# Layer 0 of a hybrid decoder step as one stream of weight products, with the delta-rule heads in between and no products inside a pair of heads

## The reference, cut to what matters

```
qkv, z, b_raw, a_raw, lx, ly = jnp.split(hn @ w_in, cuts, axis=-1)
qkv, qkv_buf_new = _causal_conv(qkv, qkv_buf, conv_qkv_w)
qkv = jax.nn.silu(qkv)
q = _l2norm(qkv[..., :GDN_QK]...) * (GDN_DK ** -0.5)
k = _l2norm(qkv[..., GDN_QK:2 * GDN_QK]...)
beta = jax.nn.sigmoid(b_raw);  g = -jnp.exp(a_log) * jax.nn.softplus(a_raw + dt_bias)
o, s_new = _gated_delta(q, k, v, beta, g, s0)
o = _rmsnorm(o, gdn_norm_g) * jax.nn.silu(z)
xb, lru_buf_new = _causal_conv(lx, lru_buf, conv_lru_w)
r = sigmoid(einsum(xblk, lru_wa) + lru_ba);  ig = sigmoid(einsum(xblk, lru_wi) + lru_bi)
log_a = -LRU_C * r * jax.nn.softplus(-lru_lambda);  a = jnp.exp(log_a)
bt = jnp.sqrt(-jnp.expm1(2.0 * log_a)) * (ig * xb)
hs = scan of h = a * h + bt;   ob = hs * jax.nn.gelu(ly)
mix = jnp.concatenate([o, ob], axis=-1) @ w_out
```

## Time and profile before

| what | value |
|---|---|
| median of 3 runs (lowest to highest) | 3324.95 us (3315.17 to 3325.36) |
| the profiled execution's own time | 3318.15 us |
| its span | 3316.3 us |
| PE busy / PEld busy | 3094.3 us (93%) / 2930.9 us (88%) |
| DVE busy / ACT busy | 1615.5 us (49%) / 1108.6 us (33%) |
| bytes moved | 456.37 MB, mean 138 GB/s |
| layer 0's mixer on PE, first product to last | 30.9 to about 866 us |

### The profile page before, as it was taken

One profiled execution on the slowest core, in us unless ns is written; L12 is line 12 of the kernel. 1 busy time (PEld: TensorE's weight loads), 2 busy tenths in 40 slices (PEclk: granted clock), 3 DMA queues, 4 the chain that ended last, 5 costly groups with the idle time before them and its releaser, 6 DMA issues.

```text
span 3316.3 us, 53710 instructions
## 1 busy us (share of the span) xinstructions
PE 3094.3 (93%) x22096; PEld 2930.9 (88%) x22096; DVE 1615.5 (49%) x1733; ACT 1108.6 (33%) x1064; POOL 110.5 (3%) x130
## 2 busy tenths in 40 slices
PE   8998649988999999999999789989999999999997
PEld 7998527768999999999999788659999999999997
DVE  5655345555644444444456543445644444444454
ACT  4323420113343333333344222333333333333343
POOL 0000000001100000000002000001100000000012
PEclk9999856779999999999999888999999999999998
DMA  6444300114555555555554242435555555555552
GB/s 189 152 141 147 95 13 27 28 40 144 151 165 165 165 165 164 164 164 165 165 163 154 84 147 61 133 104 175 149 165 165 165 165 165 164 165 164 165 165 78
DMA packets 455650, 456.37 MB, mean 138 GB/s; under 512 B 22313, under 2 KB 440170, under 8 KB 455229
## 3 DMA queue, kind: packets, MB, share of 16 engines
q1 hardware_dynamic: 455118, 455.07, 45.6%
q10 hardware_dynamic: 450, 0.16, 0.0%
HBM read 446.97 MB, written 8.22 MB: 137 GB/s over the span
## 4 chain that ended last, share of the span: by engine, by line
PE 84%; DVE 8%; ACT 4%; issue 2%; DMA 1%; SPq 1%; DVEq 0%; ACTq 0%; POOL 0%; POOLq 0%
PE ps L1238 82%; PE ps L1245 2%; ACT Wh L1268 2%; DVE Wl L1643 1%; DVE acc L1745 1%; DVE TT L1924 0%; SPq L450 0%; SPq L468 0%; DMA hrow<-in_state_lru_conv 0%; DMA gw<-in_lru_wi 0%; DMA W<-in_w_o_c 0%; DVE S L1947 0%; DVE hT L1672 0%; DVE rB L1679 0%; DVE ple L1994 0%
## 5 line engine op out<-in xcount | busy, mean ns | idle before, releaser
L1643 DVE TENSOR_TENSOR Wl<-W,Wh 128x2048 fp32r<-128x2048 f32 (+2 forms) x408 | 910.4, 2233 | 1101.5 <-ACT Wh L1268 1101.5
L1268 ACT ACTIVATE Wh<-W 128x2048 fp32r<-128x2048 f32 (+2 forms) x408 | 757.7, 1860 | 1170.8 <-PE ps L1238 1164.3
L1238 PE MATMUL ps<-Ah,Wh 128*128 128x288 f32 x3344 | 990.7, 296 | 25.2 <-DVE Wl L1643 20.2
L1238 PE MATMUL ps<-Al,Wh 128*128 128x288 f32 x3344 | 989.5, 296 | 0.0
L1238 PE MATMUL ps<-Ah,Wl 128*128 128x288 f32 x3344 | 989.5, 296 | 0.0
L1238 PE MATMUL ps<-Bh,Wh 128*128 128x288 f32 x2704 | 798.7, 295 | 10.8 <-DVE Bl L1965 10.3
L1238 PE MATMUL ps<-Bl,Wh 128*128 128x288 f32 x2704 | 799.9, 296 | 0.0
L1238 PE MATMUL ps<-Bh,Wl 128*128 128x288 f32 x2704 | 799.9, 296 | 0.0
L1238 PEld LDWEIGHTS ps<-Ah,Wh 128*128 128x128 f32 x3344 | 629.1, 188 | 30.6 <-DVE Wl L1643 30.1
L1238 PEld LDWEIGHTS ps<-Al,Wh 128*128 128x128 f32 x3344 | 630.0, 188 | 0.3
L1238 PEld LDWEIGHTS ps<-Ah,Wl 128*128 128x128 f32 x3344 | 629.4, 188 | 0.3
(11 more groups left out here) (395 smaller groups left out, 2432.6 us busy)
## 6 DMA issues: line engine op xcount, KB each, us to landing
W<-in_w_up SPq DMA_DIRECT2D x128, 1024.0 KB, 5.9
W<-in_w_down SPq DMA_DIRECT2D x128, 1024.0 KB, 5.4
W<-in_w_in_a SPq DMA_DIRECT2D x48, 1024.0 KB, 5.4
W<-in_w_ple_gate SPq DMA_DIRECT2D x32, 1024.0 KB, 5.4
W<-in_w_out_a SPq DMA_DIRECT2D x16, 1024.0 KB, 5.4
CK<-in_cache_ckv SPq DMA_DIRECT2D x64, 256.0 KB, 2.5
W<-in_w_o_c SPq DMA_DIRECT2D x16, 1024.0 KB, 5.5
W<-in_w_ukv SPq DMA_DIRECT2D x12, 1024.0 KB, 5.5
```

Source lines behind the costliest of these rows:

```text
L1238: return m.nc.tensor.matmul(out, w, x, start=start, stop=stop)
L1268: last = A(x, w, ACT.Copy)
L1643: last = TT(low, w, f(high), SUB)
```

## The change

Layer 0 becomes one list of units, `UNITS`: LX, LY, BA, then Q, K, V, Z of each pair of heads, CS (transposes of the convolution states, without a weight slot), OL (the recurrent half of `w_out`, k tiles 8 to 15) and OG (the delta-rule half, k tiles 0 to 7). On PE, ACT and DVE a generator `stream()` runs through it; one tick is six products with what belongs to them on the other engines, and `fill(n)` issues the next n ticks. All else of layer 0 stands between calls of `fill`. `TICKS` says how many ticks stand behind each step of a pair: none but at its end, `ds=57`. The whole is 532 ticks.

What comes with it: every unit of the stream uses banks 6 and 7, and PE waits for the evacuation of the unit before (`evacuated(i - 1)`); OG alternates as before. The gate matrices and `cst0` are loaded at the start, all at once. `hT` is written to DRAM (2.36 MB) at the start and read back behind slot 52, because other tiles take its place. The l2 norm is made per pair (4 rows). The staging copy of q, k, v of a pair falls away, and so does one matmul with its copy (`BB`). The scaling of `S8` and of `vb` moves from DVE to ACT, 16 small `ACTIVATE` for `S8` in each pair. DVE's split is cut in two halves of 1024. `w_out` is done in two halves, each added to `hT`. Loops over heads are written out.

```diff
+def layer0_units():
+    units, slot = [], 0
+    order = [("LX", n, 2) for n in range(4)] + [("LY", n, 2) for n in range(4)] + [("BA", 0, 2)]
+    order += [(kind, t, 2) for t in range(4) for kind in "QKVZ"]
+    order += [("CS", n, 0) for n in range(4)] + [("OL", n, 1) for n in range(8)] + [("OG", n, 1) for n in range(8)]
+    ...
+TICKS = dict(tr=0, gram=0, t1=0, q=0, tb=0, v0=0, s1=0, x1=0, v1=0, s2=0, ds=57)
...
 # PE
-    k16(S_QKV, 0, *A, m.fl_done, 0, norm=0)
-    with pe.Fori(1, 6) as t:
-        k16(S_QKV, t, *A, None, 0)
-    with pe.Fori(0, 2) as t:
-        k16(S_Z, t, *A, None, 0)
-    one_tile(S_BA, *A, None, 0, 64, 40)
-    for S in (S_LX, S_LY):
-        with pe.Fori(0, 2) as t:
-            k16(S, t, *A, None, 0)
+    def stream():
+        for i, (kind, n, s, slots) in enumerate(UNITS):
+            b, (Xh, Xl), k0, kn = 6, A, 0, 16
+            ...
+            if kind == "OG":
+                b = 2 * ((n + 1) % 2)
+                ...
+            elif i:
+                evacuated(i - 1)
+            ...
+            for half in range(slots):
+                pe.wait_ge(m.split_done, s + half + 1)
+                ...
+                for k in range(8):
+                    ...
+                    for o in range(tiles):
+                        last = products(...)
+                    if k == 7:
+                        last.then_inc(m.slot_used, 1)
+                    yield
+    fill = filler(stream())
+    fill(64)
+    fill(8)
+    pe.wait_ge(m.gw_full, 32)
+    for k in range(8):
+        ...
+        if k >= 2:
+            pe.wait_ge(m.gate_act, k - 1)
+        for g in range(2):
+            last = mm(ps[:, 2 * (k % 2) + g, 0:NT], m.gw[:, k, g, :], m.xb[:, k, :], True, True)
+        last.then_inc(m.gate_mm, 1)
+        if k % 2:
+            fill(4)
+    fill(40 + 16)
+    ...                       # lo transposed, fill(12), gate scalars transposed
+    fill(4 + 16 + 16 + 9)
...
+    def l2_norm(t):
+        pe.wait_ge(m.l2_sq, t + 1)
+        head_sums(m.sqg, (0, 1, 8, 9)).then_inc(m.l2_sum, 1)
+        fill(2)
+        fill(3)
+        pe.wait_ge(m.l2_ref, t + 1)
+        ...                   # four rows to all partitions
+        fill(2)
...
-    with pe.Fori(0, HG // 2) as t:
-        heads(t)
+    l2_norm(0)
+    for t in range(4):
+        heads(t)              # fill(TICKS[...]) behind each step, fill(57) behind the last
+        if t < 3:
+            l2_norm(t + 1)
...
+    head_sums(m.sqo, range(HG)).then_inc(m.on_sum, 1)
+    fill(11)
+    pe.wait_ge(m.on_ref, BASE["on_ref"] + 1)
...
-    k16(S_OUT, ...)           # four turns over all 16 tiles of k
+    fill(48)
+    ple_turn(0)
+    fill(16)
 # ACT, heads(t)
+        for x, P, R, Q, g, sc in both:
+            for b in range(BS):
+                at = SEQ + TS * b + TS - 1
+                last = A(g.S8[:, b, :], g.S8[:, b, :], ACT.Copy, scale=g.Eb[:, at:at + 1])
+            last.then_inc(m.g_s8, 1)
 # ACT, gates and RG-LRU
+        if k % 2:
+            fill(4)
     act.wait_ge(m.lm_done, BASE["lm_done"] + 1)
     A(m.la[:], m.lm[:, 0], ACT.Exp, scale=-1.0)
     A(m.lt[:], m.lm[:, 0], ACT.Tanh).then_inc(m.lat_done, 1)
+    fill(8)
     act.wait_ge(m.lt_done, BASE["lt_done"] + 1)
     A(m.lt[:], m.lt[:], ACT.Sqrt).then_inc(m.lroot_done, 1)
 # SP, in states()
+        small(m.gw[:, :, 0, :], a["lru_wa"][0].rearrange("k p n -> p k n"), m.gw_full)
+        small(m.gw[:, :, 1, :], a["lru_wi"][0].rearrange("k p n -> p k n"), m.gw_full)
+        small(m.cst0[:], a["cst0"], m.l_c0)
+        ...
+        small(m.hdram, m.hT[:], m.o_h)
```

More of the change, by code:

```diff
@@ L481, in states @@
         small(m.pgs[0:1, :], a["page_table"].rearrange("b n -> (b n)").unsqueeze(0), m.l_pg)
-    w = a["w_in_a"][0]
-    k16(S_QKV, w, 0, 6, first=1, then=states)
-    k16(S_Z, w, QKV, 2)
-    wv = w.rearrange("(k p) n -> p k n", p=128)
-    c0 = QKV + HG * DK
-    for i in range(2):
-        load(S_BA, i, 0, wv[:, 8 * i:8 * i + 8, c0:c0 + 16],
-             lambda x: x[:, 0:128].rearrange("p (k c) -> p k c", k=8))
-    k16(S_LX, w, c0 + 16, 2)
-    k16(S_LY, w, c0 + 16 + LRU, 2)
-    wo = a["w_out_a"][0]
@@ L555, in layer_inputs @@
         small(m.ptok[0:NS, 2, :], a["p_sample"][layer].rearrange("b t n -> (b t) n"), m.l_p)
-    layer_inputs(0)
-    with sp.Fori(1, 4) as t:
-        for i in range(4):
-            load(S_OUT, i, t, wov[:, 8 * (i % 2):8 * (i % 2) + 8, ds(t * 512 + 256 * (i // 2), 256)])
+    for kind, n, s, slots in UNITS:
+        for half in range(slots):
+            slot = s + half
+            view = (lambda x: x[:, 0:128].rearrange("p (k c) -> p k c", k=8)) if kind == "BA" else None
+            load(slot, 0, 0, weights(kind, n, half), view)
+            if slot == 3:
+                states()
+            elif slot == 24:
+                lru_out()
+            elif slot == 26:
+                old_states(0)
+            elif slot in (36, 44):
+                t = (slot - 36) // 8
+                new_states(t)
+                old_states(t + 1)
+            elif slot == 52:
+                new_states(2)
+                old_states(3)
+                hidden_back()
+            elif slot == 55:
+                conv_out()
+            elif slot == 60:
+                new_states(3)
+            elif slot == 62:
+                layer_inputs(0)
     def mlp_weights(layer, S, S_P, S_G):
@@ L830, in heads @@
             last.then_inc(m.g_tr, 1)
[L831 to L840 removed]
+            pe.wait_ge(m.g_row, 2 * t + x + 1)
@@ L917, in tensor_program @@
     pe.wait_ge(m.og_done, BASE["og_done"] + 1)
-    pe.wait_ge(m.mixl_done, 2)
+    for h in range(6, 8):
+        last = to_all(h - 6, m.rs16[0:8, :], h)
+    last.then_inc(m.on_mm, 1)
     def ple_turn(layer):
@@ L1382, in scalar_program @@
+    fill = filler(stream())
+    fill(64)
+    fill(8)
+    for k in range(8):
+        act.wait_ge(m.gate_mm, k + 1)
+        for g in range(2):
+            last = A(m.lm[:, g, k, :], ps[:, 2 * (k % 2) + g, 0:NT], ACT.Sigmoid,
+                     bias=m.par[:, k + 8 * g + C_BA:k + 8 * g + C_BA + 1])
+        last.then_inc(m.gate_act, 1)
+        if k % 2:
+            fill(4)
     act.wait_ge(m.lm_done, BASE["lm_done"] + 1)
@@ new lines, in tap @@
+    def tap(kind, n, w):
+        c, _, col, count = conv_tile(kind, n)
+        u = c % 2
+        if w == 0:
+            dve.wait_ge(m.pre_ready, c + 1)
+            dve.wait_ge(m.hist_in, c + 1)
+            if c >= 2:
+                dve.wait_ge(m.conv_act, c - 1)
+        for i in range(2):
+            g = m.par[:, i + col + count * w:i + col + count * w + 1]
+            x_w, o = m.pre[:, u, i, w:w + PRE - 3], m.acc[:, u, i, 0:PRE - 3]
+            last = STT(o, x_w, g, o, MUL, ADD) if w else TS2(o, x_w, g, None, MUL)
+        if w < 3:
+            own.after(last)
+        else:
+            last.then_inc(m.conv_done, 1)
```

1089 lines of the change are left out of this document (610 added, 479 removed).

## The result

The changed kernel takes 3314.25 us (median of 19 runs, 3306.56 to 3322.71) where before takes 3322.82 (19 runs, 3311.0 to 3326.65): a ratio of 0.9978, 95% interval 0.9968 to 0.9988. That is a gain of 0.2%, some 7 us, clear of the noise, and about a quarter of the 26.5 us forecast. The profiled execution has a span of 3307.3 us, 9.0 less than before.

A forecast was written before the change was run, and what follows sets the result against it. TensorE's products set the pace and floor (414.1 us of layer 0's mixer); the other 421.5 us could be gained. Terms sum to 809.1 against 835.6, 26.5 less, so 3318.15 becomes 3292 us, range 3255 to 3332.

The forecast's parts named there:

- the pairs: Four pairs of heads in layer 0: same chain, about 3 us less, 2.5 more for S8; 59 us each, 236 in all.
- Boundaries: Between units of the stream, PE waits for the evacuation: 1.19 us for convolved units, 1.06 for others, 32 us in all.
- restarts behind the pairs: Products behind each pair begin at the low clock: 2 us each, 7 us in all.
- the sign named: In a pair's first 10 us the clock should be above 0.9.
- the l2 norm: Four times in layer 0, waits for squares and root plus small passes: 9.9 us each, 40 in all.
- the norm of o: Behind the pairs: chain, spreading, multiplies, low halves, sums and restart take 23 us where it was 30.9.
- the RG-LRU's waits: In the three slots holding the RG-LRU's operations, PE waits 2.4 + 5.0 + 3.1 = 10.5 us.
- the scalars: Gate scalars, made on DVE and ACT behind the RG-LRU's output: PE waits 14 us for them.
- That TensorE stays slow behind each pair: Rival, chance 0.13: products behind each pair stay at the low clock, up to 146 us over four stretches; 3325 to 3360.
- That pairs run at the high clock: Rival, chance 0.20: pairs begin behind dense products and take 50 us each, 3256 us; range 3245 to 3270.
- That ScalarE and VectorE don't keep up: Rival, chance 0.17: late splits on ACT and DVE stop the stream, so no change; 3308 to 3330 us.
- the upper bounds I gave it (21, 20, 60): Most us the RG-LRU, gate scalars and l2 norm could cost if engines lag: 36.5 us more, giving 3328.

The follow-up runs named there:

- changed, second profile: The changed kernel measured once more with no edit: 3311.58 us, ratio 0.9967 to the kernel before.
- the second experiment: Scaling of S8 moved back from ScalarE to VectorE, against the changed kernel: 3295.79 us, ratio 0.9931 to the kernel before.
- six profiles against two: Six profiles with the changed kernel's pairs, summing to 246.8 to 257.0 us, against two with S8 on VectorE and no products in pairs, 238.3 and 239.5.

## Why the prediction was wrong

**The direction** was right, and so were the mechanisms outside the pairs. The naked stretch of the RG-LRU and the norms is covered, `gw` costs nothing, and what it turned into is a chain of short waits in the stream, at the places named. Boundaries (1.14 us with 0.1 behind, 30.5 in all), gates, restarts behind the pairs (2.0 us, 1.9 to 2.0 measured) and the start were sized within 1.5 us. The 1.19 us for a boundary isn't what the prediction's own parts give, though: 0.68 + 0.28 + 0.29 + 0.2 - 0.13 is 1.32, and with the overlap of the two operations in the earlier trace rows (0.60 us from start to start) 1.24, which is what was measured.

**The step that failed is the pairs**: "the chain is the same. Less: staging, ... and the clock, which is high in front now, as products run up to the pair: about 3. More: `S8` ..., 2.5 us ... 59 each, **236**". They measured 246.8 us in one profile and 253.5 in a second, 11 and 17 us over. By PE's timeline, all four pairs added up:

| part of the pairs | before | changed, first profile | changed, second profile |
|---|---|---|---|
| front, to the first level | 67.6 | 63.2 | 63.4 |
| levels | 100.2 | 100.6 | 101.6 |
| levels to last step | 48.2 | 54.6 | 60.1 |
| last step, to the next work | 22.3 | 28.4 | 28.4 |

The front is 4.3 us shorter over four pairs, where 12 were forecast. The clock does not stay high in it: in the first 10 us of the pairs it is 0.84, 0.67, 0.67 and 0.67, where the sign named was above 0.9, and in three of them it was low already on the last products in front. In pair 1 the first level gives back even this: the clock is low until 405.0 us, 25.0 after the pair's start, and was so for 22.2 us in the kernel before.

```profile
404.50:405.00 0.50, 0.50 (x4) 0.50 (x4) 0.35 (x1) 0.00 (x0) 0.00 (x0) 0.50 0.00 0
405.30:406.00 0.70, 0.70 (x8) 0.70 (x8) 0.42 (x1) 0.00 (x0) 0.00 (x0) 1.00 0.00 0
```

Behind the levels the pairs are 12 us longer in all in the first profile and 18 in the second, where 10 were forecast (2.5 each). S8 on ScalarE costs 0.30 us for each operation, not 0.16, PE waits 1.6 us for it, and behind the wait the clock is low more often; the second experiment takes 11 and 16.5 us off the same two rows (72.0 in place of 83.0 and 88.5). The chain was not quite the same either, as the section on the change says: S8 and the scaling of `vb` stand on another engine.

**A second step** was in the base. I counted layer 0's mixer to 866.5 us. The last product of `w_out` is at 862.2 in the trace of before, so 4.2 us of embeddings stood in the old sum and not in the new one. It flattered the gain. The account by the spans is then: the mixer took 825.0 us where 809.1 were forecast, 15.9 more, 10.8 of them in the pairs; the base adds 4.2; and the embeddings and what is behind gave back 2.6 that no term had. That is the 17.5 between the 26.5 forecast and the 9.0 measured.

**A third** was the rule by which I priced the work behind a wait. I took each wait at its length and small passes at the high clock or near it. In the l2 norm, eight passes of sums and eight of spreading took 5.5 to 6.1 us a time where 3.4 were priced, with 1 us or more of slow products about them; the wait for the root, priced at 2.6, was 0.4 at most (44.5 in place of 40 for all). The twelve passes that spread the rows in the norm of o took 6.1 (28 in place of 23), and the RG-LRU's waits brought 5.8 us of slow products behind them (13.3 in place of 10.5). Together 12 us, against 11 that the scalars, the start, the boundaries and the end came in below.

**The rivals.** That TensorE stays slow behind each pair did not happen: products behind a pair lose 1.9 to 2.0 us. (Its point of no gain was mis-stated: at 0.107 us each it is (26.5 + 7) / (4 x 0.107) = 78 slow products a stretch, not 68.) That pairs run at the high clock did not either, but ticks around the levels bring much of it about, in the front, the levels and the last step. That ScalarE and VectorE don't keep up forecast a time near the measured one, but not for its reason: the upper bounds I gave it (21, 20, 60) were not reached (13.3, 11.3, 44.5), and PE's waits for `Wl` are 3.3 us; the loss lay in the pairs and in the clock. A time inside the forecast range is in part luck: the terms too low and the terms too high came out of different places. The Trainium skill's rule on turning banks ("Perfetto Trace Analysis", Matmuls) holds here with a number: 22 us for about 20 boundaries, 1.1 each, although PE then waits for the split at some of them. The prediction had put it at 32 for all of them.

**What stays open.** Why the clock rises and falls at different places in pairs of the same code, worth up to 5 us a pair, is not settled: it is only seen in the windows. That S8's wait acts through the clock is argued from six profiles against two and from the windows, not shown by itself; it could be a change of order on VectorE as well. The share of the ticks' gain that is clock and the share that is idle time of PE filled can't be split in front of the levels, where both are.

## What to carry to other kernels

In a stream of dense products, price a wait of PE of 2 us or more at nearly double (here 1.6 to 2.5 us on top), price the small matmuls behind it at the low clock, and look for the instruction that causes it even if the wait is only 1.6 us long. Sixteen small operations on ScalarE ahead of a copy that PE needs took 4.8 us here where VectorE took 2.4 in two; price such operations from a row of the same shape and not by width. Taking one wait away is worth nothing until you have looked at what the engine behind it waits for: here 6.5 us less for the squares put 7.3 us on the root. If a chain of short steps can't be hidden whole, put the independent products in front of its dense part and not only behind the chain, and give the filling work a second pair of output banks.

## What the runs showed of the hardware

A stretch of 73 small matmuls in the same order takes 13.4 to 16.3 us, at a granted clock of 0.78 and 0.66, in two executions of one kernel; PE's idle time in it is 1.6 and 2.1 us, so most of the difference is clock. PE was busy for 21.6 of the first 25.2 us of pair 1 at a mean clock of 0.57. Products in dense order stand 0.24 us apart at first behind a wait of 2.0 us as they do behind a pair of 60 us, and lose 1.6 to 2.0 us in either case. Behind waits of 4.8 us they lost 2.5 us in one place and 1.6 in another; behind a wait of 1.0 to 1.5 us they lose 0.1. An `ACTIVATE` of 128 by 128 with a scale takes 0.30 us of ScalarE in a row of sixteen, where one of 128 by 2304 takes 2.1: 2.5 times its share by width, 0.12.
